# A 31-tap convolution moved from GpSimd to VectorE in part, and the chunk order of a token mixer rearranged

## What is computed

```python
proj = xn @ w_in + b_in     # c_a, c_b, p_u, m_q, m_k, m_v, m_z, m_i, m_f, g_pre
u = c_a * sigmoid(c_b)
u = causal_depthwise_conv(u, conv_dw_w, conv_dw_b)      # 31 taps, 512 channels
y_a = silu(layer_norm(u, ...)) @ w_conv_out
y_b = pool_mixer(p_u, pool_w, pool_scale) @ w_pool_out
qk = silu(causal_depthwise_conv([m_q, m_k], ...))       # 4 taps, 2048 channels
h = mlstm_chunkwise(q, k * dh**-0.5, v, ig, lf)         # 4 heads of 256
y_c = (head_norm(h) * mlstm_norm_g * sigmoid(m_z)) @ w_mlstm_out
g = sigmoid(g_pre)
y = (g[0] * y_a + g[1] * y_b + g[2] * y_c) @ w_out
```

## Time and profile before

| | |
|---|---|
| runs of the kernel | 2267.55, 2268.95, 2272.57 us, median 2268.95 |
| profiled execution, its own time as its span from first to last instruction | 2267.0 us |
| TensorE busy | 2101.9 us, 93% |
| VectorE busy | 1685.5 us, 74% |
| ScalarE busy | 1279.7 us, 56% |
| GpSimd busy | 236.1 us, 10% |

### The profile page before, as it was taken

How to read it: one execution, slowest core, us unless ns; L and a number is a source line. 1 busy time by engine, 2 the same in 40 slices (tenths; PEclk the granted TensorE clock), 3 DMA queues, 4 the chain that set the end, 5 groups by cost and what they waited for, 6 DMA issues and landing times.

```text
span 2267.0 us, 33302 instructions
## 1 busy us (share of the span) xinstructions
PE 2101.9 (93%) x12896; PEld 1895.8 (84%) x12896; DVE 1685.5 (74%) x1570; ACT 1279.7 (56%) x1105; POOL 236.1 (10%) x195
## 2 busy tenths in 40 slices
PE   6778999999998778899997999999999999999997
PEld 5778899989998778899986888888888888888885
DVE  5899655545445899655547888888888888888885
ACT  3434544434334434554435767777777767777774
POOL 0990000000000990000000000000000000000000
PEclk8889999999999888999997999999999999999998
DMA  5334445544554334444534989999898989999893
GB/s 180 112 112 154 144 136 166 168 126 158 181 183 148 112 112 154 145 138 164 167 131 166 370 319 365 355 324 387 305 377 310 373 316 367 350 333 371 313 380 121
DMA packets 309483, 526.71 MB, mean 232 GB/s; under 512 B 13542, under 2 KB 156550, under 8 KB 309382
## 3 DMA queue, kind: packets, MB, share of 16 engines
q1 hardware_dynamic: 309382, 525.29, 66.3%
HBM read 524.21 MB, written 1.05 MB: 232 GB/s over the span
## 4 chain that ended last, share of the span: by engine, by line
PE 76%; DVE 17%; ACT 3%; issue 3%; DMA 0%; DVEq 0%; ACTq 0%; POOL 0%; SPq 0%
PE ps L1461 23%; PE ps L1463 23%; PE ps L1462 23%; DVE w_lo L987 5%; DVE cacc L1037 3%; DVE c L1054 2%; DVE cacc L1039 2%; PE ps L1829 1%; ACT w_hi L664 1%; PE ps L1774 1%; PE ps L1508 1%; PE ps L1841 1%; ACT w_hi L671 1%; PE ps L1595 1%; PE ps L1575 1%
## 5 line engine op out<-in xcount | busy, mean ns | idle before, releaser
L987 DVE TENSOR_TENSOR w_lo<-raw,w_hi 128x2048 fp32r<-128x2048 f32 x330 | 762.6, 2313 | 380.9 <-ACT w_hi L664 318.1
L1461 PE MATMUL ps<-w_hi,a_hi 128*128 128x512 f32 (+1 forms) x1472 | 571.3, 388 | 20.9 <-DVE w_lo L987 20.0
L1463 PE MATMUL ps<-w_hi,a_lo 128*128 128x512 f32 (+1 forms) x1472 | 563.3, 383 | 0.0
L1462 PE MATMUL ps<-w_lo,a_hi 128*128 128x512 f32 (+1 forms) x1472 | 562.8, 382 | 0.0
L1461 PE MATMUL ps<-a_hi,w_hi 128*128 128x256 f32 x1520 | 446.7, 294 | 50.4 <-DVE w_lo L987 34.9
L664 ACT ACTIVATE w_hi<-raw 128x2048 fp32r<-128x2048 f32 x159 | 301.0, 1895 | 319.0 <-PE ps L1463 311.3
L1462 PE MATMUL ps<-a_lo,w_hi 128*128 128x256 f32 x1520 | 440.2, 290 | 0.0
L1463 PE MATMUL ps<-a_hi,w_lo 128*128 128x256 f32 x1520 | 439.4, 289 | 0.0
L671 ACT ACTIVATE w_hi<-raw 128x2048 fp32r<-128x2048 f32 x171 | 328.0, 1918 | 116.1 <-PE ps L1463 116.1
L1461 PEld LDWEIGHTS ps<-a_hi,w_hi 128*128 128x128 f32 x1520 | 302.3, 199 | 53.7 <-DVE w_lo L987 36.2
L1461 PEld LDWEIGHTS ps<-w_hi,a_hi 128*128 128x128 f32 x1472 | 280.0, 190 | 79.5 <-DVE w_lo L987 25.5
(11 more groups left out here) (265 smaller groups left out, 2427.0 us busy)
## 6 DMA issues: line engine op xcount, KB each, us to landing
raw<-in_moe_w SPq DMA_DIRECT2D x171, 1024.0 KB, 6.5
raw<-in_w_in SPq DMA_DIRECT2D x68, 1024.0 KB, 5.2
mem_t<-in_moe_w SPq DMA_DIRECT2D x56, 1024.0 KB, 6.1
area<-in_moe_w SPq DMA_DIRECT2D x56, 1024.0 KB, 6.0
xf<-in_moe_w SPq DMA_DIRECT2D x56, 1024.0 KB, 5.8
raw<-in_ffn_w SPq DMA_DIRECT2D x33, 1024.0 KB, 5.2
raw<-in_w_mlstm_out SPq DMA_DIRECT2D x8, 1024.0 KB, 4.9
raw<-in_w_out SPq DMA_DIRECT2D x8, 1024.0 KB, 5.0
```

The source lines that it names most:

```text
L987: return dve.tensor_tensor(dst, whole, as_f32(hi), ALU.subtract)
L1461: pe.matmul(dst, wh, xh, start=start, stop=False, skip_group_check=True)
L1462: pe.matmul(dst, wh, xl, start=False, stop=False, skip_group_check=True)
L1463: return pe.matmul(dst, wl, xh, start=False, stop=stop, skip_group_check=True)
```

## The change

- Of the 31-tap convolution GpSimd keeps block 0 alone (128x256 products and sums, in `xf` blocks 4 and 5); VectorE has blocks 1, 2 and 3. Its taps are given out by a table of counts from chunk 2 to chunk 32.
- The chunk order is a list `MIX`, and what follows a chunk goes by its kind instead of its number. q and k chunks stand in turns with v, z and pooling chunks. `conv4` goes by the order q0, k0, q1, k1, ...
- `SCORES` is (11, 15, 19, 23), and TensorE waits only for the q, k and v of the head in hand.
- The branches are merged in the order pooling, mLSTM, convolution. The hidden transposes follow chunk 29, the hidden split chunk 30, the layer norm's sums chunks 34 and 36. The mLSTM's gate and out-projection are four and four; `w_conv_out` is the last pair ahead of `w_out`.
- The pooling's partial sums lie in `xf` instead of `dec` and `wdk`.

```diff
+MIX = [("cb", 0), ("ca", 0), ("cb", 1), ("ca", 1)]
+MIX += [("q", 0), ("v", 0), ("k", 0), ("v", 1), ("q", 1), ("v", 2), ("k", 1), ("v", 3)]
+MIX += [("q", 2), ("z", 0), ("k", 2), ("pu", 0), ("q", 3), ("pu", 1), ("k", 3), ("z", 1), ("z", 2), ("z", 3), ("pw", 0)]
+MIX += [("gb", i) for i in range(4)] + [("wp", i) for i in range(2)]
+MIX += [("gc", i) for i in range(4)] + [("wm", i) for i in range(4)]
+MIX += [("ga", i) for i in range(4)] + [("wc", i) for i in range(2)]
...
-SCORES = (PW - 3, PW - 1, PW, PW + 1)
-GATE_ROWS = QK0
-LN_MEAN, LN_VAR, HIDDEN_T = WP0 + 1, GA0 + 1, GA0
+SCORES = (11, 15, 19, 23)
+GATE_ROWS = AT["q", 0]
+HIDDEN_T = AT["gc", 0]
+HIDDEN_SPLIT = AT["gc", 1]
+LN_MEAN, LN_VAR = AT["wm", 1], AT["wm", 3]
-DVE_TAPS = {j: range(3 * (j - V0), min(3 * (j - V0) + 3, CONV_K)) for j in range(V0, V0 + (CONV_K + 2) // 3)}
+def tap_plan():
+    count = {2: 3, 3: 3, 5: 3, 7: 3, 9: 3, 11: 3, 13: 4, 15: 4, 19: 4, 20: 4, 21: 3, 22: 1, 23: 3, 24: 3, 25: 2, 26: 2, 27: 2, 28: 2, 29: 3,
+             31: 3, 32: 4}
+    todo = [(0, k) for k in range(6)]
+    for k in range(CONV_K):
+        todo += [(1, k)] + ([(0, k + 6)] if k + 6 < CONV_K else [])
+    plan = {}
+    for j, n in count.items():
+        plan[j], todo = todo[:n], todo[n:]
...
-                for c in range(2):
-                    last = ch.did(pool.tensor_scalar(c31[:, c, :], u_pad[:, c, 0:T], col(1, c), col(0, R_CB + c), ALU.mult, ALU.add))
-                total = c31[:, 0:2, :]
+                total = c31[:, 0, :]
+                last = ch.did(pool.tensor_scalar(total, u_pad[:, 0, 0:T], col(1, 0), col(0, R_CB), ALU.mult, ALU.add))
                 for k in range(1, CONV_K):
-                    tap = par[:, 1, k * CB:k * CB + 2].rearrange("p (c o) -> p c o", o=1).broadcast_to([P, 2, T])
+                    prod = xf[:, 4 + k % 2, :]
+                    tap = par[:, 1, k * CB:k * CB + 1].broadcast_to([P, T])
                     ch.need(last)
-                    ch.link(pool.tensor_tensor(taps[:, k % 2], u_pad[:, 0:2, k:k + T], tap, ALU.mult))
-                    ins = pool.tensor_tensor(total, total, taps[:, k % 2], ALU.add)
+                    ch.link(pool.tensor_tensor(prod, u_pad[:, 0, k:k + T], tap, ALU.mult))
+                    ins = pool.tensor_tensor(total, total, prod, ALU.add)
...
-                for k in DVE_TAPS.get(j, ()):
-                    marks = tap_marks
-                    for i in range(2):
-                        c = 2 + i
+                for pair, k in TAPS.get(j, ()):
+                    dve.wait_ge(u_done.sem, u_done.at(layer, pair + 1))
+                    for c in ((1,), (2, 3))[pair]:
...
 def merge(layer, j, n, parts):
                 multiplied(layer, j)
+                if n == 2:
+                    dve.wait_ge(c31_pool.sem, c31_pool.at(layer, 1))
...
-                if WC0 <= j < GC0:
-                    merge(layer, j, 4 + 2 * (j - WC0), 2)
-                if j == GC0 - 1:
+                if j == HIDDEN_SPLIT:
...
-                if GC0 <= j < WO0 and (j - GC0) % 2:
-                    merge(layer, j, 8 + (j - GC0) // 2, 1)
-                if j == WO0 - 2:
-                    for q in range(3):
+                if kind == "wm":
+                    merge(layer, j, 4 + i, 1)
+                if kind == "wc":
+                    merge(layer, j, 8 + 2 * i, 2)
+                    for q in (2 * i, 2 * i + 1):
                         merged_lo(layer, q)
...
-                pe.wait_ge(qk_done.sem, qk_done.at(layer, 8))
+                pe.wait_ge(qk_done.sem, qk_done.at(layer, 2 * hd + 2))
...
-                pe.wait_ge(v_done.sem, v_done.at(layer, HEADS))
+                pe.wait_ge(v_done.sem, v_done.at(layer, hd + 1))
```

More of the change, by code:

```diff
@@ L89, in bank_plan @@
 def bank_plan():
[L92 to L96, removed]
+    steps = []
+    for c, (kind, i) in enumerate(MIX):
+        steps.append((("chunk", c), 2 if kind in ("pw", "wp", "wc") else 1))
+        if c == HIDDEN_T:
+            steps.append(("hidden_t", 4))
     plan, last, n = {}, [None] * 4, 0
@@ L198, in trunk @@
         rows = z_sig[0:HEADS, 0:4, :]
-        taps = xf[:, 0:4, :].rearrange("p (s c) t -> p s c t", s=2)
+        pool_sums = [xf[:, 2 * i:2 * i + 2, :].rearrange("p a b -> p (a b)") for i in range(2)]
         m_row = sb("m_row", [HEADS, T])
@@ L609, in _ @@
                 pool.memset(t, 0.0).then_inc(e_const, 1)
-        GATE_NO = {c: n for n, c in enumerate([*range(GB0, WP0), *range(GA0, WC0), *range(GC0, WO0, 2)])}
+        GATE_NO = {AT[kind, q]: 4 * n + q for n, kind in enumerate(("gb", "gc", "ga")) for q in range(4)}
         def bank(key, part=0):
@@ L620, in read_by @@
             c = key[1]
[L621 to L632, removed]
+            kind, i = MIX[c]
+            if kind in ("q", "k"):
+                return qk_pre, QK_NO[c] + 1
             if c in GATE_NO:
                 return gate_done, GATE_NO[c] + 1
[L635 to L643, removed]
+            if kind == "wp":
+                return gate_used, 2 * i + part + 1
+            if kind == "wm":
+                return gate_used, 4 + i + 1
+            if kind == "wc":
+                return y_done, 2 * i + part + 1
+            return {"cb": b_sig, "ca": u_done, "v": v_done, "pu": pool_pre, "z": z_done, "pw": pw_done, "wo": h_mix, "xk": xk_done,
+                    "xv": xv_done, "xq": xq_done, "xo": h_att}[kind], i + 1
         def flat(a):
@@ L771, in post @@
             def post(layer, j):
[L773 to L776, removed]
+                kind, i = MIX[j]
+                if j in QK_NO:
+                    qk_input(layer, QK_NO[j])
+                elif kind == "cb":
                     if i:
@@ L810, in post @@
                     act.activation(small[:, STD:STD + 8], small[:, SS:SS + 8], ACT.Sqrt, bias=eps[:, 0:1], scale=1.0 / DH).then_inc(hid_std.sem, 1)
+                if j == HIDDEN_SPLIT:
+                    for i in range(4):
+                        act.wait_ge(hid_gated.sem, hid_gated.at(layer, i + 1))
+                        act.activation(b_hi[:, 2 * i:2 * i + 2, :], k_t[:, 2 * i:2 * i + 2, :], ACT.Copy).then_inc(hid_hi.sem, 1)
                 if j == LN_MEAN:
@@ L821, in post @@
                     act.wait_ge(ln_silu.sem, ln_silu.at(layer, 1))
+                    multiplied(layer, AT["wm", 3])
                     act.activation(b_hi[:, 4:8, :], c31[:, :, :], ACT.Copy).then_inc(ln_hi.sem, 1)
[L823 to L830 removed]
+                if kind == "wc":
+                    for q in (2 * i, 2 * i + 1):
                         merged_hi(layer, q)
[L832 to L833 removed]
                 if j == WO0:
@@ L1166, in post @@
                     ins.then_inc(v_done.sem, 1)
-                if j < QK0 and (j - AB0) % 2:
-                    i = (j - AB0) // 2
+                if kind == "ca":
                     multiplied(layer, j)
@@ L1196, in post @@
                     ins.then_inc(hid_nrm.sem, 1)
-                if WP0 <= j < GA0:
-                    merge(layer, j, 2 * (j - WP0), 2)
+                if kind == "wp":
+                    merge(layer, j, 2 * i, 2)
                 if j == LN_MEAN:
```

166 lines of the change are left out of this document (74 added, 92 removed).

## The result

The changed kernel takes 2212.05 us (median of 4 runs, 2211.37 to 2215.92) against 2269.12 us; the ratio is 0.9753, 95% interval 0.9739 to 0.9767. That is 57 us less. The forecast was 2181, 88 less, with a range of 2160 to 2222: the direction is right, and the gain is two thirds of what was forecast. That the time lies in the range is owed to the width of the range: its upper end came from the starved case (2206), and that case did not come.

The account below looks back on a forecast made before the run. VectorE was taken to bound both mixers' input projections. Loss a layer falls from 61.7 us to 17.8 (8.6 + 2.8 + 4.4 + 2), gaining 43.9, or 87.8 in two layers: 2181 us, range 2160 to 2222.

Parts of the forecast that it names:

- starved case: Rival: VectorE holds its turn, GpSimd's convolution falls behind, head 0's mask waits; 21 us lost, 2206 us; chance 0.20.
- Bound: Both mixers' input projections: VectorE is the bound, and layer 0 loses 61.7 us there.
- Part 1: GpSimd's convolution at half width: 1.5 us a pair, 45 us instead of 75; alternating VectorE instructions 0.75 instead of 1.33.
- same-price case: Rival: half-width GpSimd pairs stay at 2.5 us, contending VectorE instructions at 1.33; gain 20 us, 2249; chance 0.08.
- Part 2: 31 more taps on VectorE: 12.4 us a layer, those behind pool_w costed at nothing.
- Part 3: Alternated chunks, splits 7 to 11: VectorE 15.9 us late, 7.3 of cover, loss 8.6; GpSimd ends at about 119.
- From split 12 to 20: Mixer stretch after the contended one: VectorE 54.8 us against TensorE's 59.1, pooling at most 7 late, so covered.
- Part 4: Heads' scores four chunks apart: wdk waits (5.3 + 1.1) go; VectorE's new waits for exp and mask taken as 0.
- Part 5: Convolution branch last: b_lo's 1.7 us goes, hidden transposes wait 2.8 instead of 5.0, last merge 4.4 against 4.8.
- Lower clock: Matmuls at 1.2 GHz after pauses: 16.6 us of layer 0's loss before, 2 a layer after two short pauses.
- the 8.6: TensorE's loss from VectorE's lateness in the contended stretch, 8.6 us a layer, said to hold its own lower clock.
- 264.4: TensorE's estimated work in us from the split of chunk 3 to that of chunk 46, against 326.1 elapsed.

Follow-up runs that it names:

- e2: Changed kernel with the convolution blocks split as before (0 and 1 on GpSimd, 2 and 3 on VectorE), in the new chunk order; 2254.44 us.
- e9: Changed kernel with q and k chunks in a row again and the heads' scores behind chunks 19, 21, 22, 23; 2237.66 us.
- e8: Changed kernel with block 0 on VectorE too, so all four blocks there and GpSimd without convolution; 2207.23 us.
- e6: Changed kernel with ScalarE's squares of a head's hidden rows one chunk later, behind its split of the next weights; 2196.40 us.
- e4: Changed kernel with GpSimd doing one tap of block 0 and 29 of its 31 taps left out of the computation; 2196.63 us.
- e3: Changed kernel with the heads' scores behind chunks 19, 21, 22, 23 as before; 2214.60 us.
- e11: Changed kernel, hidden-row squares one chunk later, VectorE's merge behind w_conv_out chunks ahead of its next split, head transposes waiting for their own banks; 2182.45 us.
- e13: Changed kernel, hidden-row squares one chunk later, all four blocks on VectorE, VectorE's merge behind w_conv_out chunks ahead of its next split; 2172.84 us.
- e5: Changed kernel with the pooled input's split (high and low part) behind chunk 19 instead of 20; 2213.75 us.

## Why the prediction was right in direction and too large in size

**Bound (rows 1, 2, 5): right.** VectorE was the bound of the projections, and e2 and e9 show that neither the order nor the blocks alone carry the gain (14 and 30 of 57 us).

**Part 1, half the width: right.** A pair takes 1.52 us with gaps for 1.5 forecast, alternating 1.63; a multiply-add beside it 0.84 for 0.75. The two one-input steps take 0.73 without contention, 0.37 each for 0.27. GpSimd's last sum ends at 119.5 for "about 119". It won its turn as at the start of the old trace, so neither the starved case nor the same-price case came.

**Part 2, the taps: right in price, not wholly free behind pool_w.** Six take 2.45 us. The 24 entries behind pool_w are 39 multiply-adds, not 36. They were costed at nothing, but they stand in VectorE's queue ahead of the pooling merge, whose bank TensorE waits 2.2 us for; e8, with more of them, waits 3.9.

**Part 3, the contended stretch: right.** From split 3 to 12 it is 69.6 us against 54.7 of TensorE: 14.9 late for 15.9. TensorE lost 5.1 on w_lo in the mixer for 8.6.

**The step that failed: "From split 12 to 20 I get 54.8 us on VectorE ... covered."** The nine splits with what follows them took 61.6 (116.23 to split 21 at 177.78). Two handovers of 3.06 are 6.1 of these 6.8, and my sum had VectorE's own work only, none of its waits for ScalarE. So at split 21 VectorE was 14.9 + 61.6 - 59.1 = 17.4 us behind TensorE's undisturbed count, where the forecast's own terms give 15.9 + 54.8 - 59.1 = 11.6, and the sum has no term for what followed: 4.9 at pool_w, 2.6 at the numerators, 2.2 at the bank. e6, which removes all four handovers of a layer, prices them at 15.7 us, half of the 31 us that were missing; in it pool_w waits 1.8 us, the numerators 1.7, the bank 0.8. The wait at pool_w is not this lateness alone, for it also stands in e4, where VectorE is on time at split 12 and the handovers are in place.

**Part 4: the wrong wait was bounded.** I weighed VectorE's wait for exp and mask, taken as 0, and it was within 1 us. I didn't weigh ScalarE's wait for VectorE's hidden rows, which moves with `SCORES` in the same way and stands ahead of a split. By e3 spacing the heads is worth nothing clear; the forecast gave it 6.4 us a layer. TensorE's wait at the scores did go; 2.6 us at the numerators are left.

**Part 5: mis-sized, and before was misread.** "4.8 of the 7.6 for a_lo at the last merge" is the wait at the layer's start; at the last merge the kernel before waits 2.85:

```profile
370.08 0.39 PE L1461 MATMUL ps<-a_hi,w_hi 128*128 128x256 f32 x1 [2.85 <-DVE a_lo L987]
```

The changed kernel waits twice there, 1.97 and 3.10, so there is 2.2 us a layer more of idle time at the last merge, where I had a gain of 0.4:

```profile
332.43 0.36 PE L1453 MATMUL ps<-a_hi,w_hi 128*128 128x256 f32 x1 [1.97 <-DVE a_lo L986]
...
339.85 0.39 PE L1453 MATMUL ps<-a_hi,w_hi 128*128 128x256 f32 x1 [3.10 <-DVE a_lo L986]
```

Merge first (e11) left 1.1 of these 5.1. The transposes' wait is 4.3 for 2.8, for a table load of 1.28 us lies between ScalarE's split and its sigmoid there, which I left out.

**Lower clock: mis-sized.** I gave 2 us a layer to it after the change, and let the 8.6 hold its own. By the same reckoning as before (busy time less 264.4) it is 11.4. With the 5.1 for w_lo that is 16.5 where my two terms have 10.6, so 6 us a layer are missing here. That it is clock in the main shows over the kernels: beyond the 264.4 TensorE is busy 18.5 us at a granted clock of 0.93 (before), 11.4 at 0.97 (changed) and 4.4 at 0.99 (e13). From 220 to 270 us, where TensorE's pauses now stand, the changed kernel has 0.93. In e5 the pauses got shorter and the clock lower, so less idle time didn't by itself bring the clock back.

In sum layer 0's stretch loses 35.6 us (24.2 idle, 11.4 busy beyond the work) where the forecast had 17.8.

What stays open: how the 7.8 us a layer of e6 divide among the handovers. In layer 0 its stretch is 9.5 us shorter, 4.8 of them by split 21 and the rest behind it, where the other two handovers stood; TensorE is idle 6.9 us less and busy 2.5 less. No run removes the handovers and GpSimd's contention together while VectorE keeps three blocks.

## What to carry to other kernels

When work is moved into the stage of the late engine, add up its waits for other engines as well as its work: look in each other engine's queue for what stands between the moved result and the next thing the late engine needs, and move that behind it. A wait of TensorE that disappears without the time getting shorter (e5) says that an engine upstream is late; look for its idle time, not for the waits. And read where in time a wait stands before taking it as a term: the longest a_lo wait was in another place than I had put it.

## What the runs showed of the hardware

Where both read SBUF, VectorE and GpSimd mostly take turns, one instruction each: beside products and sums of 128x512 a multiply-add of VectorE takes 1.33 us, beside those of 128x256 0.84, alone 0.41, while GpSimd's own products and sums beside these multiply-adds lengthen only from 0.61 to 0.68 and from 0.75 to 0.80. So narrower instructions on GpSimd are cheaper for VectorE even at the same number of them. A longer instruction of VectorE costs GpSimd more: beside a split of 128x2048 a product takes 2.54 and a sum 2.66. And the turns are not always kept: at 110.78 in the kernel before, six multiply-adds ran at 0.41 each while one sum of GpSimd took 5.87. What decides between the two is open.

VectorE's gate scans contend too, on 4 partitions only. The forecast had counted three of its five steps as contending, not the two scans. The same scan in the kernel before, in the changed one, and in e4, where GpSimd is idle:

```profile
100.72 1.63 DVE L1020 TENSOR_TENSOR_SCAN z_sig<-zrow,z_sig 4x256 f32<-4x256 f32 x1
```

```profile
87.00 1.11 DVE L1019 TENSOR_TENSOR_SCAN z_sig<-zrow,z_sig 4x256 f32<-4x256 f32 x1
```

```profile
84.03 0.68 DVE L1019 TENSOR_TENSOR_SCAN z_sig<-zrow,z_sig 4x256 f32<-4x256 f32 x1
```
